# A hybrid decoder trunk on one core: GLU projections ahead of q, k and v, fourteen weight jobs turned from channel form into row form, and the second group's heads placed earlier

## The reference

```python
# every layer: h = h + W_out(concat(gated branches(RMSNorm(h))))
# even layer: one input projection feeds
#  A) gated DeltaNet, 8 heads of 128: causal conv (4 taps) on q, k, v, SiLU, l2 norm,
#     per-head decay, chunked delta rule; RMS norm; times SiLU(zA)
#  B) GLU (a * sigmoid(b)) -> causal depthwise conv, 31 taps, 1024 channels
#     -> LayerNorm -> swish; times SiLU(zB)
#  M) cross-attention, 4 heads of 256, into the memory tokens; times SiLU(zM)
# odd layer:
#  C) stick-breaking attention, 16 heads of 128; times SiLU(z)
#  M) the memory cross-attention again; times SiLU(z)
S_t = exp(g_t) (I - beta_t k_t k_t^T) S_{t-1} + beta_t k_t v_t^T ;  o_t = q_t S_t
```

## Time and profile before

| | |
|---|---|
| median of three runs | 1370.07 us |
| the profiled execution | 1368.7 us |
| its span | 1367.0 us |
| granted TensorE clock, mean | 0.999 |
| PE / PEld busy | 99% / 88% |
| DVE / ACT / POOL busy | 66% / 53% / 8% |
| weights and the rest read from HBM | 234 MB, 174 GB/s over the span |

### The profile page before, as it was taken

One profiled execution on the slowest core, in us unless ns is written; L12 is line 12 of the kernel. 1 busy time (PEld: TensorE's weight loads), 2 busy tenths in 40 slices (PEclk: granted clock), 3 DMA queues, 4 the chain that ended last, 5 costly groups with the idle time before them and its releaser, 6 DMA issues.

```text
span 1367.0 us, 20681 instructions
## 1 busy us (share of the span) xinstructions
PE 1353.8 (99%) x8187; PEld 1209.3 (88%) x8187; DVE 907.1 (66%) x1334; ACT 730.7 (53%) x1120; POOL 104.6 (8%) x104
## 2 busy tenths in 40 slices
PE   8999999999999999999999999999999999999998
PEld 8999899998988988888888898898898898998887
DVE  5458689897898988755656454665655736556663
ACT  6545633476335545675446455756746657654341
POOL 2000301003010101000002020020110200000000
PEclk9999999999999999999999999999999999999999
DMA  9555564555646855654455664564564554544652
GB/s 311 174 179 169 150 189 134 153 165 158 213 123 184 280 189 179 196 174 148 152 171 165 201 192 143 185 205 138 168 203 150 192 178 144 196 154 139 200 185 77
DMA packets 134505, 239.47 MB, mean 175 GB/s; under 512 B 13920, under 2 KB 19977, under 8 KB 134409
## 3 DMA queue, kind: packets, MB, share of 16 engines
q1 hardware_dynamic: 131689, 233.43, 53.9%
q10 hardware_dynamic: 2720, 4.72, 1.0%
HBM read 234.32 MB, written 3.80 MB: 174 GB/s over the span
## 4 chain that ended last, share of the span: by engine, by line
PE 97%; DVE 1%; DMA 0%; issue 0%; POOL 0%; ACT 0%; SPq 0%; DVEq 0%; ACTq 0%
PE job L1640 18%; PE job L1642 18%; PE job L1641 18%; PE job L1646 11%; PE job L1648 11%; PE job L1647 11%; PE mixer L1685 3%; PE mixer L1881 1%; PE mixer L1901 1%; PE mixer L1789 1%; PE mixer L1919 1%; PE mixer L1770 1%; PE mixer L1932 1%; PE mixer L1719 0%; DVE cvr L1503 0%; DMA raw<-in_ev_w_in_dram 0%
## 5 line engine op out<-in xcount | busy, mean ns | idle before, releaser
L1263 DVE TENSOR_TENSOR wlo<-raw,whi 128x1024 fp32r<-128x1024 f32 x432 | 530.0, 1250 | 126.1 <-ACT whi L917 118.5
L917 ACT ACTIVATE whi<-raw 128x1024 fp32r<-128x1024 f32 x431 | 446.5, 1055 | 205.1 <-PE job L1642 102.6
L1640 PE MATMUL job<-whi,xhi 128*128 128x512 f32 x1088 | 437.4, 402 | 0.0
L1642 PE MATMUL job<-whi,xlo 128*128 128x512 f32 x1088 | 424.8, 390 | 0.0
L1641 PE MATMUL job<-wlo,xhi 128*128 128x512 f32 x1088 | 423.9, 390 | 0.0
L1646 PE MATMUL job<-xhi,whi 128*128 128x256 f32 x1272 | 365.1, 287 | 0.0
L1648 PE MATMUL job<-xhi,wlo 128*128 128x256 f32 x1272 | 359.9, 283 | 0.0
L1647 PE MATMUL job<-xlo,whi 128*128 128x256 f32 x1272 | 359.8, 283 | 0.0
L1646 PEld LDWEIGHTS job<-xhi,whi 128*128 128x128 f32 x1272 | 243.8, 192 | 0.3
L1647 PEld LDWEIGHTS job<-xlo,whi 128*128 128x128 f32 x1272 | 243.9, 192 | 0.1
L1648 PEld LDWEIGHTS job<-xhi,wlo 128*128 128x128 f32 x1272 | 243.7, 192 | 0.0
(11 more groups left out here) (275 smaller groups left out, 983.8 us busy)
## 6 DMA issues: line engine op xcount, KB each, us to landing
raw<-in_od_w_in_dram SPq DMA_DIRECT2D x160, 512.0 KB, 4.6
raw<-in_ev_w_in_dram SPq DMA_DIRECT2D x143, 512.0 KB, 4.2
raw<-in_ev_w_out_dram SPq DMA_DIRECT2D x48, 512.0 KB, 4.5
raw<-in_od_w_out_dram SPq DMA_DIRECT2D x48, 512.0 KB, 4.6
raw<-in_w_mem_kv_dram SPq DMA_DIRECT2D x32, 512.0 KB, 4.1
reg<-in_mem_dram ACTq DMA_DIRECT2D x4, 512.0 KB, 6.2
hid<-in_x_dram ACTq DMA_DIRECT2D x4, 512.0 KB, 8.0
out_dram<-hid SPq DMA_DIRECT2D x4, 512.0 KB, 2.7
```

Source lines behind the costliest of these rows:

```text
L917: act(whi[:, c % RING, :, :], raw[:, c % RAWS, :, :], ACT.Copy).then_inc(s_hi, 1)
L1263: vec.tensor_tensor(wlo[:, c % RING, :, :], raw[:, c % RAWS, :, :], whi[:, c % RING, :, :].bitcast(F32), ALU.subtract).then_inc(s_lo, 1)
L1640: mm(out_, xh, hi, start=first, stop=False)
L1642: return mm(out_, xl, hi, start=False, stop=last)
```

## The change

1. **Order of the jobs.** The even layer had q, k, v, GLU a, GLU b, zA for group 0, then the same for group 1. It now has a, b, q, k, v, zA, then a, q, k, v, b, zA.
2. **Forms.** `CHANNEL` has q, k, v of both groups (6 jobs of 8 chunks). The other fourteen are row jobs. What needs channels is turned by PE: `gT` (8 steps, the GLU product, then a copy by ACT) and `zT` (40 steps, in place of the ten `gz`: two transposes, an ACT copy and an ACT tanh of 256 columns, a DVE product of 256 columns). All of them use `M[3]`. The second `rrow` goes.
3. **DeltaNet heads.** `dnC` has the six taps of q and k, and may start after the k job. `dnW` has the three taps of v (each waits for the one before), `dnX` and `dnY` their tanh and product. The tanh now goes to SBUF. The second group's heads begin in the labels of the first group's `d5` steps: `dnC4` in 76, `dnW4` in 82, `dnB4` in 87 (before: `dnC4` in 77 and the last of `dnB` in 89, with `d70` in 76; `d70` is now in 86).
4. **The inverse**: `inC` stands one label after `inF` and `inD` two later (before: both three after `inF`).
5. **`ba`** is 32 matmuls (a 48-row stationary operand), `bat` two matmuls with `pick`.
6. **Conv and layer norm.** The first taps come at label 22 (before 45), the layer norm in labels 137 to 157 (before 160 to 181), beside `zT8` to `zT15`. The added jobs from `J_OM` to the one before `J_ODIN` are added one label sooner.
7. **Start and end.** `first` is followed by two more warm-up matmuls, the second half of chunk 0 is split after `xt1` (`half`), and `open` has the row form. The last chunk is multiplied token half by token half, and each half is added and stored by itself.

```diff
 def _jobs():
-    for g in range(2):
-        for base in (Q0, K0, V0, GA0, GB0, ZA0):
-            JOBS.append(("ev_in", 0, base + 512 * g, KT, 0))
+    for base, g in ((GA0, 0), (GB0, 0), (Q0, 0), (K0, 0), (V0, 0), (ZA0, 0), (GA0, 1), (Q0, 1), (K0, 1), (V0, 1), (GB0, 1),
+                    (ZA0, 1)):
+        JOBS.append(("ev_in", 0, base + 512 * g, KT, 0))
...
-GATE_JOBS = [J_ZB, J_ZB + 1, J_ZM, J_ZM + 1] + [J_ODIN + 4 * g + 3 for g in range(4)] + [J_ODIN + 18, J_ODIN + 19]
-CHANNEL = sorted([0, 1, 2, 3, 4, 6, 7, 8, 9, 10] + GATE_JOBS)
+CHANNEL = [2, 3, 4, 7, 8, 9]
...
-WARM = 8
+WARM, WARM_MORE = 8, 2
...
-INV_STEP = (3.0, 3.0)
+INV_STEP = (1.0, 2.0, 3.0)
...
-        for h in range(h0, h0 + 4):
-            s += [(("dnC", h), 1)] + ([(("dnB", h - 1), 0)] if h > h0 else [])
-            s += [(("dnS", h), 1), (("dnU", h), 1)]
-        s += [(("dnB", h0 + 3), 1), (("dnV", g), 2), (("dnR", g), 2.5)]
+        s += [(("dnV", g), 2), (("dnR", g), 2.5)]
...
-        s += [(("inW", g), 0), (("inA", g), 0), (("inB", g), 2), (("inF", g), INV_STEP[0]), (("inC", g), 0), (("inD", g), INV_STEP[1])]
+        s += [(("inW", g), 0), (("inA", g), 0), (("inB", g), 2), (("inF", g), INV_STEP[0]), (("inC", g), INV_STEP[1]), (("inD", g), INV_STEP[2])]
...
-    stream(0, -1, [(("xt", 0), 0), (("xt", 1), 0), (("open", 0), 0), (("xt", 2), 0), (("xt", 3), 0)])
+    stream(0, -1, [(("xt", 0), 0), (("xt", 1), 0), (("half", 0), 0), (("open", 0), 0), (("xt", 2), 0), (("xt", 3), 0)])
...
+    def heads(g, a, b, c):
+
+        for q in range(4):
+            h = 4 * g + q
+            stream(1, a + 2 * q, [(("dnC", h), 1), (("dnS", h), 1), (("dnU", h), 0)])
+            stream(1, b + q, [(("dnW", h), 1), (("dnX", h), 1), (("dnY", h), 0)])
+            stream(1, c + q, [(("dnB", h), 0)])
+        return c + 4
...
-    p = stream(1, after(J_V[0]), work)
+    p = stream(1, heads(0, after(J_K[0]), after(J_V[0]), after(J_V[0]) + 3), work)
...
-    start = max(int(p) + 3, after(J_V[1]))
-    p = stream(1, start, work)
+    a = max(after(J_K[1]), row_of("d5c", 0) + 1)
+    b = max(after(J_V[1]), a + 5)
+    p = stream(1, heads(1, a, b, max(b + 3, row_of("d7", 0) + 1)), work)
...
-        stream(2, after(J_GLU[g] + 1) + 6 * g, [(("glu", g), 0)])
-    stream(3, max(after(J_ZB + 1), int(inverted) + 1), [(("gz", 0), 3), (("gz", 1), 0)])
-    q = stream(3, max(after(J_ZM), oa), [(("gz", 2), 2)])
-    q = stream(3, max(after(J_ZM + 1), q), [(("gz", 3), 1)])
+        stream(2, after(J_GLB[g]), [(("glu", g), 2 + g)] + [(("gT", ct), 1) for ct in range(4 * g, 4 * g + 4)])
+    stream(3, max(after(J_ZB + 1), int(inverted) + 1), [(("zT", n), 1) for n in range(8)])
+    q = stream(3, max(after(J_ZM), oa), [(("zT", n), 1) for n in range(8, 12)])
+    stream(3, max(after(J_ZM + 1), q), [(("zT", n), 1) for n in range(12, 16)])
...
-        late = 5 if j == J_GLU[1] + 1 else 0 if j in (J_ODIN - 1, len(JOBS) - 1) else 1 if j else 3
+        late = 0 if J_OM <= j < J_ODIN or j == len(JOBS) - 1 else 1 if j else 3
...
-    left, behind, p = list(range(4 * TAPS)), 0.0, after(J_GLU[0] + 1) + 3
+    left, behind, p = list(range(4 * TAPS)), 0.0, after(J_GLB[0]) + 3
...
-            if p < after(J_GLU[pr // 2] + 1) + 6 * (pr // 2) + 2:
+            if p < after(J_GLB[pr // 2]) + 4 + 2 * (pr % 2):
...
+                if j == len(JOBS) - 1:
+                    for t in range(T):
+                        sp.wait_ge(s_evD, evac_done(j)[1] + t)
+                        sp.dma_start(out[128 * t:128 * t + 128, 512 * b:512 * b + 512], hid[:, t, 512 * b:512 * b + 512]
+                                     ).then_inc(s_out, 16)
+                        stores += 16
+                    continue
...
-                sc.wait_ge(*evac_done(J_V[h // 4]))
+                sc.wait_ge(*evac_done(J_K[h // 4]))
...
-                for c in range(3):
+                for c in range(2):
...
+            def do_dnW(h):
+                sc.wait_ge(*evac_done(J_V[h // 4]))
+                if h >= 4:
+                    sc.wait_ge(s_back, h - 3)
+                col = V_CONV + 24 * (CONV - 1) + dn_tile(h, 2)
+                act(ykqv[:, h % 4, 2, :], dn_source(h, 2), ACT.Copy, scale=vt[:, col:col + 1]).then_inc(s_tap, 1)
+
+            def do_dnX(h):
+                sc.wait_ge(s_cv4, taps_done["dnW", h])
+                if h >= 2:
+                    sc.wait_ge(s_silu, silu_done["dnY", h - 2])
+                act(scr[:, S * (h % 2):S * (h % 2) + S], ykqv[:, h % 4, 2, :], ACT.Tanh, scale=0.5).then_inc(s_th, 1)
...
             def do_dnS(h):
-                sc.wait_ge(s_cv4, 9 * h + 9)
-                for q in bank_free["dnS", h]:
-                    sc.wait_ge(*q)
+                sc.wait_ge(s_cv4, taps_done["dnC", h])
+                if h:
+                    sc.wait_ge(s_silu, silu_done["dnU", h - 1])
                 y = ykqv[:, h % 4, :, :]
...
-                act(M[2 * (h % 2)][:, :].rearrange("p (c s) -> p c s", c=2), y[:, 0:2, :], ACT.Tanh, scale=0.5)
-                act(M[2 * (h % 2) + 1][:, 0:S], y[:, 2, :], ACT.Tanh, scale=0.5).then_inc(s_th, 1)
+                act(mix[:, 0:2, :], y[:, 0:2, :], ACT.Tanh, scale=0.5).then_inc(s_th, 1)
...
-            def do_gz(q):
-                sc.wait_ge(*evac_done(GATE_JOBS[q]))
...
+                kt = zsource(n)[3]
+                sc.wait_ge(s_zp, n + 1)
...
-                dst, z = gate_place(q)
-                act(dst, z, ACT.Tanh, scale=0.5).then_inc(s_zc, 1)
+                act(mix[:, kt, :], M[3][:, 0:S], ACT.Copy)
+                act(M[3][:, S:2 * S], M[3][:, 0:S], ACT.Tanh, scale=0.5).then_inc(s_zc, 1)
...
+            def do_dnW(h):
+                ve.wait_ge(s_tap, first_taps["dnW", h])
+                n = taps_done["dnW", h] - 3
+                y = ykqv[:, h % 4, 2, :]
+                for r in range(1, CONV):
+                    col = V_CONV + 24 * (CONV - 1 - r) + dn_tile(h, 2)
+                    if r > 1:
+                        ve.wait_ge(s_cv4, n)
+                    vec.scalar_tensor_tensor(out=y[:, r:], in0=dn_source(h, 2)[:, 0:S - r], scalar=vt[:, col:col + 1],
+                                             in1=y[:, r:], op0=ALU.mult, op1=ALU.add).then_inc(s_cv4, 1)
+                    n += 1
+
+            def do_dnY(h):
+                ve.wait_ge(s_th, tanh_done["dnX", h])
+                y = ykqv[:, h % 4, 2, :]
+                vec.scalar_tensor_tensor(out=y, in0=scr[:, S * (h % 2):S * (h % 2) + S], scalar=1.0, in1=y, op0=ALU.add,
+                                         op1=ALU.mult).then_inc(s_silu, 1)
...
+                if c == NCH - 1:
+                    for t in range(T):
+                        for k in (2 * i, 2 * i + 1):
+                            ins = three(pj[j % 2][t][:, :], SLOT[fill + k], t, whi[:, c % RING, k % 2, :],
+                                        wlo[:, c % RING, k % 2, :], k == 0, k == kts - 1)
+                        ins.then_inc(s_pe, 1)
+                    return
...
                 for k in range(KT):
-                    for a, b in ((bah, xhi), (bal, xhi), (bah, xlo)):
-                        ins = mm(M[0][0:16, 0:S], a[:, k, :], b[:, k, :], start=(k == 0 and a is bah and b is xhi),
-                                 stop=(k == KT - 1 and b is xlo))
+                    mm(M[0][0:48, 0:S], bas[:, k, 0:48], xhi[:, k, :], start=(k == 0), stop=False, skip_group_check=True)
+                    ins = mm(M[0][0:16, 0:S], bas[:, k, 0:16], xlo[:, k, :], start=False, stop=(k == KT - 1), skip_group_check=True)
...
+            def do_zT(n):
+                j, slot, col, _ = zsource(n)
+                pe.wait_ge(*evac_done(j))
+                take("zT", n)
+                for t in range(T):
+                    ins = turn(M[3][:, 128 * t:128 * t + 128], proj[:, slot, t, 128 * col:128 * col + 128])
+                ins.then_inc(s_zp, 1)
```

More of the change, by code:

```diff
@@ L602, in banks, with counted @@
                     "d4x": [0],
-                    "d5a": [0], "d5b": [1], "d5c": [2], "d5d": [0], "d5e": [1], "rrow": [3],
+                    "d5a": [0], "d5b": [1], "d5c": [2], "d5d": [0], "d5e": [1], "gT": [3], "zT": [3], "rrow": [3],
                     "lnm": [3], "lns": [3], "mas": [0], "mat": [1], "sbT": [0], "sbz": [1], "sbo": [2]}.get(step, [])
+        def counted(units):
+            n, at = 0, {}
+            for st in plan:
+                if st[0] in units:
+                    n += units[st[0]]
+                    at[st] = n
+            return at
+        first_taps, taps_done = counted({"dnC": 1, "dnW": 1}), counted({"dnC": 6, "dnW": 3})
+        tanh_done, silu_done = counted({"dnS": 1, "dnX": 1}), counted({"dnU": 1, "dnY": 1})
         def inv_count(i):
@@ L981, in do_rrow @@
             def do_rrow(n):
[L982 to L985 removed]
+                sc.wait_ge(s_vp, 3)
+                act(rrow[:, :], M[3][:, 0:S], ACT.Copy).then_inc(s_vt, 1)
             def do_baw(_):
@@ L1343, in do_dnC @@
             def do_dnC(h):
-                ve.wait_ge(s_tap, h + 1)
```

(16 more changed lines are left out.)

207 lines of the change are left out of this document (114 added, 93 removed).

## The result

The changed kernel takes **1373.31 us**, the median of 16 runs (1372.18 to 1374.28). The kernel before, run 16 times beside it, takes 1370.13 us (1368.95 to 1371.58). The ratio is 1.0022 with a 95% interval of 1.0015 to 1.0029: slower by 3 us, where 4 us faster was forecast, and 0.8 us above the upper end of the range. The profiled execution has 1374.02 us, a span of 1372.3 us and a mean granted clock of 0.996. It is one of the longer ones: 3 of the 16 have 0.996, 5 have 0.997 and 8 have 0.998.

What follows compares the result with a forecast made beforehand. PE, busy 99% of the span, was taken as the bound: what it issues plus its waits. The terms summed to -3.8 against the profiled 1368.7 us, giving 1364.9, or 1366.3 as the median; range 1357.0 to 1372.5.

Steps and rivals of the forecast that it cites:

- Term 5: Labels 80 to 88: DVE's work ahead of `gate0` ends late, so PE waits, mostly at `d70`: +9.6 us, bounds 4.5 and 14.
- Term 4: Mid kernel: PE's waits around the inverse and one late `xt` all go: -4.7 us, bounds -3.5 and -4.7.
- terms 1 and 2: 111 chunks go from channel to row form, -17.8 us; 48 transpose pairs between row chunks +12.0, moved steps +0.7.
- term 3: `ba` and `rrow`: 16 fewer matmuls at 0.12 and one `rrow` of four small matmuls at 0.4: -2.3 us.
- Other new waits: `zT` through one bank, PE to ACT to DVE and back, hidden unless other steps are ahead: +1.5 us, bounds 0 and 3.
- Start and end: `xt0` comes sooner as ACT makes `vt` first, -1.6 us; half the last addition beside PE and a shorter store, -1.2.
- A: Labels 80 to 88: DVE keeps up, no jam, the new waits there are nil: 1356.7 us, chance 0.18.
- the stick-breaking rival C: Stick-breaking heads: `zT` work on ACT and DVE makes 16 heads each 0.5 us late: +8, or 1374; chance 0.08.
- B: Labels 80 to 88: all of `dnW4` to `dnW7` wait, +4.2, and the jam drops PE's clock, +3.4: 1374 us, chance 0.12.
- The prediction's own test: PE's idle time in labels 80 to 88: under 3 us means A, over 13 with a clock below 1 means B.

Runs made afterwards that it cites:

- run 16: Not a run's label: the words are from "run 16 times", the kernel before, unchanged, measured beside the changed kernel: 1370.13 us.
- the last run: Changed kernel with v taps later, d6's last operation at the gate, reload behind store, job 9's copy in label 83, `ba` one label after `baw`: 1358.50 us, ratio 0.9913.

## Why the prediction was wrong

**Wrong in sign, right in the places.** The sum was -3.8, and the two profiled executions are 5.3 us apart the other way. Two steps failed most. Term 5 had its waits right (9.6, measured 9.3 us) and put the clock behind them at nothing: the stretch lost 12.5 us. Term 4 had all the waits of mid kernel go (-4.7), but 2.2 us stayed ahead of the two first `d4x`, since the reload lands late: -2.3. The rest is in sizes: -5.1 for terms 1 and 2, where about -3.2 came out, and -2.3 for term 3, where -0.9 did. Term by term, in the profiled executions:

1. *Channel to row, and the transposes* (terms 1 and 2, -17.8 + 12.7 = -5.1): about -3.2. From the first matmul of chunk 1 to that of the last chunk the last run is 7.0 us shorter than the kernel before. Its waits there are 2.1 us for 4.5, and `ba` is 1.4 of it (term 3), which leaves 3.2. Right in sign, 1.9 too large. The price of a chunk was 0.126 in place and not 0.16, but I had put the difference into the transposes. In the odd layer the two cancel: the chunks of the six gate jobs take 5.4 us less, and the other chunks, among them those with the `zT`, 5.7 us more. So the part of the change that was worked out at -17.8 brings little.
2. *`ba` and `rrow`* (-2.3): about -1.4, and a new wait of 0.5 ahead of `ba`, up to 1.4 in other runs. DVE has two copies of `pick` to make there first, which I had counted nowhere.
3. *Waits that go* (-4.7): -2.3. **This step failed.** I read the wait as one of issue alone, and moved the reload forward in the queue without asking what stands ahead of it. Two weight chunks do, and it lands 7.8 us after its issue instead of 4. With the reload right behind its store both waits are gone, in the changed kernel and in the kernel before. `inD` should stay behind `inC`, as it did before.
4. *New waits in labels 80 to 88* (+9.6): the idle times are 1.6 at `d5d`, 6.4 at `d70`, none at `d72` and 1.3 at `dnB5`, 9.3 us. The walk gave 1.4, 6.1, 0.9 and 1.2. Right, and the run with the v taps later shows its cause. But chunks 80 to 93 take 54.3 us, and 42.7 in the last run, which has 0.8 of idle time left there. The whole is 12.5. **The clock is what was left out**, 2.0 us in the trace. **This step failed too.** The last 1.2 us are not split further.
5. *Other new waits* (+1.5): `zT` alone never waited. A chunk with one takes 2.97 us as with any pair. In its place came `lnm` behind POOL (1.3). Right in size by accident.
6. *Start and end* (-1.6, -1.2): chunk 1 starts at 12.45 for 14.20, and from the last matmul's start to the span's end it is 4.0 for 4.9 us. So -1.75 and -0.9. Right, though the start is not that fixed: in the second profile of the kernel before, chunk 1 starts at 14.99.

These add up to 4.7 of the 5.3 us. The last 0.6 are in none of them.

**The rivals.** A and the stick-breaking rival C did not happen (`sbc` has no idle time). B was priced at 1374 and the result is 1373.3, but its point was off: "it decides from a jam of about 16 us on". A single idle stretch of 6.4 us was enough for a fallen clock, as were 4.6 and 2.9 us in later runs, and my forecast already had one of 6.1. So B's clock belonged into the sum, at least as a term with a bound. I had one row that spoke against it (2.4 us at 195 without a loss) and one for it (the start), and I took the first for longer waits as well. The other half of B, every `dnW` late behind `dnX` on ACT, was half there: two of the four waited, 0.55 and 1.47 us.

**The base.** The sum was made against 1368.7, with 1.4 added for the median. That shift is there, and 1.2 us of it go with the mean clock of 69 executions. The profile of the changed kernel is off the other way, 0.7 us above its median. So the profiles are 5.3 us apart and the medians 3.2. One profile does not show what most executions do.

The prediction's own test, "if over 13 with a clock below 1 behind it, B", points to what happened, with 9.3 us of idle time in place of 13.
